# Turning 128-row tiles with an ordinary product against the identity in a two-block transformer kernel

## The reference

```python
x = first_block(x, mem, ...)          # mixers + squared-relu FFN
for i in range(2):                    # second_block
    x = x + 0.5 * swiglu(rmsnorm(x, ffn_norm1[i]), wg, wu, wd)
    h = rmsnorm(x, mix_norm[i])
    x = x + (sliding_window_attention(h, ...) if i == 0 else latent_attention(h, ...))
    x = x + 0.5 * swiglu(rmsnorm(x, ffn_norm2[i]), wg, wu, wd)
```

## Time and profile before

| | us |
|---|---|
| median of 3 runs | 1296.6 |
| lowest and highest | 1295.24, 1297.97 |
| profiled execution, its own time | 1299.77 |
| its span | 1298.0 |
| TensorE busy | 1236.5 (95%) |
| VectorE busy | 886.6 (68%) |
| ScalarE busy | 611.1 (47%) |
| mean granted TensorE clock | 0.979 |

### The profile page before, as it was taken

How to read it: one execution, slowest core, us unless ns; L and a number is a source line. 1 busy time by engine, 2 the same in 40 slices (tenths; PEclk the granted TensorE clock), 3 DMA queues, 4 the chain that set the end, 5 groups by cost and what they waited for, 6 DMA issues and landing times.

```text
span 1298.0 us, 17912 instructions
## 1 busy us (share of the span) xinstructions
PE 1236.5 (95%) x7062; PEld 1065.0 (82%) x7062; DVE 886.6 (68%) x1078; ACT 611.1 (47%) x786; POOL 158.7 (12%) x164
## 2 busy tenths in 40 slices
PE   7998899999899999979999999999999869999998
PEld 7995799999788888866888888888888757888887
DVE  4886565565676776675866776866776475866675
ACT  5556534344443444576543444444344485544342
POOL 2431212012210000240100000100001340100000
PEclk9998899999999999999999999999999889999999
DMA  9773268695685556452555565655553313555530
GB/s 295 223 214 98 67 168 207 163 246 165 172 283 181 191 194 193 145 167 77 190 183 181 191 194 162 201 190 182 182 179 121 122 33 99 194 184 182 185 129 33
DMA packets 165401, 219.62 MB, mean 169 GB/s; under 512 B 13676, under 2 KB 143792, under 8 KB 165212
## 3 DMA queue, kind: packets, MB, share of 16 engines
q1 hardware_dynamic: 155356, 212.28, 51.8%
q0 software_dynamic: 9984, 6.49, 2.9%
HBM read 213.26 MB, written 5.25 MB: 168 GB/s over the span
## 4 chain that ended last, share of the span: by engine, by line
PE 85%; DVE 8%; ACT 4%; issue 1%; POOL 1%; DMA 0%; SPq 0%; DVEq 0%; ACTq 0%
PE ps L276 26%; PE ps L251 14%; PE ps L253 14%; PE ps L252 14%; PE ps L278 13%; DVE w_lo L232 2%; PE ps L555 1%; POOL scratch L799 1%; ACT w_hi L225 1%; PE ps L580 1%; PE ps L568 1%; ACT h_both L436 1%; DVE h_both L444 1%; DVE arena L658 1%; DVE scratch L806 0%
## 5 line engine op out<-in xcount | busy, mean ns | idle before, releaser
L225 ACT CAST w_hi<-raw 128x2048 fp32r<-128x2048 f32 x197 | 374.1, 1899 | 431.5 <-PE ps L278 274.3
L232 DVE TENSOR_TENSOR w_lo<-raw,w_hi 128x2048 fp32r<-128x2048 f32 x194 | 443.1, 2285 | 170.5 <-ACT w_hi L225 169.7
L276 PE MATMUL ps<-h_both,w_hi 128*128 128x512 f32 x1408 | 500.0, 399 | 4.6 <-DVE h_both L444 4.6
L278 PE MATMUL ps<-h_both,w_lo 128*128 128x256 f32 x1408 | 395.2, 281 | 0.0
L276 PEld LDWEIGHTS ps<-h_both,w_hi 128*128 128x128 f32 x1408 | 265.2, 188 | 70.6 <-issue 5.5
L278 PEld LDWEIGHTS ps<-h_both,w_lo 128*128 128x128 f32 x1408 | 266.5, 189 | 1.4
L251 PE MATMUL ps<-w_hi,act_hi 128*128 128x512 f32 x480 | 188.3, 392 | 1.4 <-DVE act_lo L1047 1.4
L253 PE MATMUL ps<-w_hi,act_lo 128*128 128x512 f32 x480 | 187.4, 390 | 0.0
L252 PE MATMUL ps<-w_lo,act_hi 128*128 128x512 f32 x480 | 187.2, 390 | 0.0
L283 DVE TENSOR_REDUCE arena<-ps 128x512 f32<-128x1024 f32 x88 | 107.8, 1225 | 82.4 <-PE ps L278 82.1
L251 PE MATMUL ps<-w_hi,h_both 128*128 128x256 f32 (+3 forms) x324 | 110.6, 341 | 10.2 <-DVE h_both L444 5.0
(11 more groups left out here) (237 smaller groups left out, 1300.9 us busy)
## 6 DMA issues: line engine op xcount, KB each, us to landing
raw<-in_ffn_wg SPq DMA_DIRECT2D x44, 1024.0 KB, 5.4
raw<-in_ffn_wu SPq DMA_DIRECT2D x44, 1024.0 KB, 5.4
raw<-in_ffn_wd SPq DMA_DIRECT2D x44, 1024.0 KB, 4.9
raw<-in_w_ff SPq DMA_DIRECT2D x32, 1024.0 KB, 17.2
raw<-in_w_in SPq DMA_DIRECT2D x8, 1024.0 KB, 11.8
raw<-in_a_w_in SPq DMA_DIRECT2D x5, 1024.0 KB, 5.4
raw<-in_w_out SPq DMA_DIRECT2D x4, 1024.0 KB, 5.1
raw<-in_a_w_out SPq DMA_DIRECT2D x4, 1024.0 KB, 5.0
```

Source lines behind the costliest of these rows:

```text
L225: nc.scalar.copy(w_hi[:, b % RING, 0:n], raw[:, b % RAW, 0:n]).then_inc(hi_ready, 1)
L232: nc.vector.tensor_tensor(w_lo[:, b % RING, 0:n], raw[:, b % RAW, 0:n], w_hi[:, b % RING, 0:n].bitcast(F32), ALU.subtract).then_inc(lo_rea ...
L276: nc.tensor.matmul(ps[:, bank + f, :], hi[:, k, f * P:(f + 1) * P], h_both[:, k, :, :].rearrange("p a b -> p (a b)"), start=k == 0, stop=F ...
L278: last = nc.tensor.matmul(ps[:, bank + f, 0:TOK], lo[:, k, f * P:(f + 1) * P], h_both[:, k, 0, :], start=False, stop=k == KD - 1, skip_gro ...
```

## The change

A helper `turned` issues an ordinary matrix product with the tile as the stationary operand and `ident` as the moving one, and takes the place of `nc.tensor.transpose` at nine call sites. Order, operands, PSUM places and semaphores are the same. The core of the diff:

```diff
+        def turned(to, source):
+            return nc.tensor.matmul(to, source, ident[:, :], start=True, stop=True, skip_group_check=True)
...
-                        last = nc.tensor.transpose(ps[:, turn_bank(n) + k // 2, col:col + P], x[:, t, k * P:(k + 1) * P], ident[:, :])
+                        last = turned(ps[:, turn_bank(n) + k // 2, col:col + P], x[:, t, k * P:(k + 1) * P])
...
-                        last = nc.tensor.transpose(ps[:, 2 + h.e % 2, col:col + P], h.weights(t)[:, s * P:(s + 1) * P], ident[:, :])
+                        last = turned(ps[:, 2 + h.e % 2, col:col + P], h.weights(t)[:, s * P:(s + 1) * P])
...
-                nc.tensor.transpose(ps[0:QK, 6 + h % 2, t * P:(t + 1) * P], qb[:, t, h * QK:(h + 1) * QK], ident[:, :])
-                last = nc.tensor.transpose(ps[0:QK, 6 + h % 2, TOK + t * P:TOK + (t + 1) * P], kc[:, t, h, :], ident[:, :])
+                turned(ps[0:QK, 6 + h % 2, t * P:(t + 1) * P], qb[:, t, h * QK:(h + 1) * QK])
+                last = turned(ps[0:QK, 6 + h % 2, TOK + t * P:TOK + (t + 1) * P], kc[:, t, h, :])
...
-                nc.tensor.transpose(ps[:, 7 - g // 4 * 2, g % 4 * P:(g % 4 + 1) * P], ws[:, g, :], ident[:, :])
+                turned(ps[:, 7 - g // 4 * 2, g % 4 * P:(g % 4 + 1) * P], ws[:, g, :])
...
-                            last = nc.tensor.transpose(ps[:, A_TURN_BANK[p], k * TOK + t * P:k * TOK + (t + 1) * P], source, ident[:, :])
+                            last = turned(ps[:, A_TURN_BANK[p], k * TOK + t * P:k * TOK + (t + 1) * P], source)
```

More of the change, by code:

```diff
@@ L1912, in gated_turn @@
                         for t in range(TT):
-                            last = nc.tensor.transpose(ps[:, 6 + k // 2, k % 2 * TOK + t * P:k % 2 * TOK + (t + 1) * P],
-                                                       oa[:, t, k * P:(k + 1) * P], ident[:, :])
+                            last = turned(ps[:, 6 + k // 2, k % 2 * TOK + t * P:k % 2 * TOK + (t + 1) * P],
+                                                       oa[:, t, k * P:(k + 1) * P])
                     last.then_inc(oa_psum, 1)
@@ L2039, in turn_latent @@
                             col = (k - chunks[0]) * TOK + t * P
-                            last = nc.tensor.transpose(ps[:, bank, col:col + P], cn[:, t, k * P:(k + 1) * P], ident[:, :])
+                            last = turned(ps[:, bank, col:col + P], cn[:, t, k * P:(k + 1) * P])
                     last.then_inc(c_turned, 1)
```

## The result

The changed kernel takes 1312.72 us (median of 4 runs, 1311.32 to 1315.34) against 1297.01 (1295.24 to 1297.97): a ratio of 1.0123, 95% interval 1.0096 to 1.015. It is slower by 15.7 us, inside the range of the forecast (1312 to 1334) but only 0.7 us above its lower edge; 25.9 were forecast. One execution of the kernel before, beside the later experiments, took 2445.9 us and is left out of every figure here.

What follows compares the result with a forecast made beforehand. TensorE was taken as the bound (busy 1236.5 of 1298.0 us, 85% of the last chain). Borders 6.7, M1 3.5, MA 5.6 and MB 10.1 sum to 25.9 us, added to 1296.6 for 1322.5 us; range 1312 to 1334.

Steps and rivals of the forecast that it cites:

- The price of a turn: Each ordinary turn on TensorE takes two passes, 224 ns against 109: 115 ns more, 213 more at half clock.
- a price of four passes: Rival on the price of each turn: four passes, sixteen turns taking 7 us; chance 0.02.
- The borders: Turns of x at the seven borders between stages: early ones delay the path, others are hidden; together 6.7 us.
- M1: First attention: half-clock turns 1.2 us, next eight 0.2, last three groups of six 2.1; 3.5 us in all.
- MA: Second attention: turns ScalarE waits for, groups partly covered by busy ScalarE, last four groups on TensorE's chain; 5.6 us.
- MB: Third attention, the largest term: loop steps, last groups, waits ahead of the steps and latent turns; 10.1 us.
- the closed loop: In MB's attention, 11 of a step's 14 turns lie on a 4.42 us loop: 1.27 us more each, five steps 6.35.
- The clock: Rival: more passes keep TensorE's clock from falling after 100 us, at most 20.9 us back, 1301.6 us; chance 0.07.
- One sign of being wrong: In the profile after, the half-clock stretches would be gone; the prediction expected them to stay.
- its own forecast: The main case for the whole kernel, 1322.5 us, own range 1316 to 1329, chance 0.73.
- half of the 19.2 us in the attentions hidden: Rival: other engines cover half the cost of M1, MA and MB; 16.3 us added, 1312.9 us; chance 0.11.

Runs made afterwards that it cites:

- e4_qk: Kernel before, with ordinary products only for the 64 turns of q and k in MB: 1302.32 us, ratio 1.0051.
- e1_twice: Kernel before, with each of the 344 turns kept a transpose and issued twice into the same place: 1311.98 us, ratio 1.0127.
- e5_fill: Kernel before, all transposes, the last turn of x at each border repeated while TensorE waits (10 times; 8 at F1, fewer at F0): 1291.84 us, ratio 0.9961.
- e7_fill_half: As e5_fill with 5 repeats in place of 10 (5 and 4 at F1, 1 and 1 at F0): 1292.64 us, ratio 0.995.
- e2_borders: Kernel before, with ordinary products only in the 112 turns of x at the seven borders between stages: 1297.98 us, ratio 1.0004.
- e3_inner: Ordinary products in M1, MA and MB, transposes at the seven borders, against the kernel before: 1315.45 us, ratio 1.0136.
- e6_fill_mb: As e5_fill, plus twelve repeated transposes in each of two hidden places of MB: 1289.34 us, ratio 0.9927 to the kernel before.

## Why the prediction was right, and where it was not

- **The price of a turn: right.** Two rows at 112 ns in place of one at 109, 344 rows more. The row of L375 was the very form: 16 products, 32 rows, 3.74 us. At half clock two rows cost 0.425 us (in the turn of x before F0 the tenth ends 2.13 us behind the first start and the eighteenth 3.83), where 0.427 was worked out. No run shows a price of four passes, which has a chance in the prediction: at four times 109 ns the sixteen turns would have taken 7 us, and they took 3.73.
- **The borders: right** to 0.1 us in sum (6.7 forecast, 6.8 measured), the early turns on the path and the late ones hidden.
- **M1: right** in sum, 3.8 against 3.5, with two parts that offset: the first two groups added 1.65 at ScalarE's copies (1.2 forecast), the next eight turns 0.95 where 0.2 was said, and the last three groups, with what follows them, 1.2 in place of 2.1.
- **MA: mis-sized**, 4.6 against 5.6. The four turns at 554 and at 561 us cost 0.48 and 0.50 as said. From 570 to 586 us 1.0 was added where 1.9 was forecast, so more than half is covered there, presumably by ScalarE, which is still busy for 18.8 of 20 us there (571.8 to 591.8 in the changed kernel); the last four groups gave 2.45 for 2.8.
- **MB: right**, a step of 5.63 against 5.69, the closed loop as described, 9.2 + 0.5 against 10.1. e4_qk took it apart: eight of the turns alone add 0.87.
- **The clock: the step that failed.** The sum took it as unchanged, and its return had a chance of 0.07, because the stretch behind 1001 us is full of thin products and no row showed that more passes lift the clock. Neither was a reason against it: that stretch begins a few microseconds behind a border. 11.75 us came back behind 100 us in the profiled execution (2.4 + 1.35 + 8.0), and about 9 in the medians (24.9 - 15.7). That is 9.2 of the 10.2 us between 25.9 and 15.7; the other 1.0 is path cost, most of it in MA. The bound of that rival, 20.9 us back, held. The mechanism was named and priced, but left out of the sum as if it were all or nothing; half of it would have given 1312. One sign of being wrong, that the half-clock stretches are gone, came true for two thirds of them.
- **The range: luck.** The measured 1312.7 lies outside the range that the prediction gives to its own forecast (1316 to 1329). The wider range went down to 1312 to take in another case, half of the 19.2 us in the attentions hidden, 1312.9. The number of that rival is the nearest of all, and its mechanism is wrong: the path cost of M1, MA and MB is 18.1 us, not 9.6.
- **A misreading without effect.** The 8s of the clock line for MB stand in slices 32 and 33, for M1 in 4 and 5; the sum uses neither.
- **Why the clock came back** is shown in part. Not the kind of pass (e1_twice); passes put into waiting time at the borders give part of it back with no other change (e5_fill, e7_fill_half); ordinary turns at the borders alone pay for themselves (e2_borders), and without them the clock stays low (e3_inner, with few runs, and e4_qk). The changed kernel still has a higher clock than e2_borders (0.988 to 0.992 against 0.984 to 0.992, median 0.986), so the borders are not all of it. The runs of one kernel scatter as well (0.973 to 0.987 for the kernel before). How the chip decides no run shows.

## What to carry to other kernels

An fp32 turn by an ordinary product cost a second pass here (224 ns in place of 109), so keep the transpose instruction wherever others wait for the result; it pays to ask of each group which turns are waited for, since over a third of the added time here was hidden (39.6 us on TensorE, 24.9 on the path). When an edit lengthens or shortens TensorE's work beside its waits, read the clock by stage before summing: here the granted clock (0.988 to 0.992, above every run of before) returned about 9 of the 24.9 us. And where TensorE waited between dense stages (1.05 us before F1, 1.28 before MA), repeating a harmless turn there was worth 0.4 to 0.7% of this kernel, with intervals that reach from 0.1 to 1.0%.

## What the runs showed of the hardware

- An ordinary fp32 product of 128 columns left two rows of MATMUL, 112 ns apart at full clock (the 16 turns of x before MA: 32 rows in 3.73 us); a transpose of the same tiles left one, at 109 ns (16 rows in 1.91 us). Eight turns made ordinary inside a loop of waits (e4_qk) add 0.87 us, 0.109 each.
- Adding transposes raised the mean granted clock as much as ordinary passes did: 0.988 to 0.993 (e1_twice) against 0.988 to 0.992 (the change), where the kernel before had 0.973 to 0.987.
- Repeats in TensorE's idle time raised the clock, and the matched starts of e5_fill show nothing added at any border: in the profile of e6_fill_mb the latent part of MB has a mean clock of 0.91 for 0.80, and the stretch at half clock behind F1 is in none of the profiles with repeats; the kernels with repeats (e5_fill, e7_fill_half, e6_fill_mb) became 5.8, 5.0 and 8.3 us faster with more work on TensorE.
